# Value products in groups of six units, eight tiles of exponentials and a ring of three score banks in two of a kernel's three attentions

## The chip, the cores and the metric

The kernel runs on one core of one Trainium2 chip. The metric is device time in microseconds (us). Its engines are TensorE (PE; its weight loads are PEld), VectorE (DVE), ScalarE (ACT), GpSimd (POOL) and SyncE (SP, which issues DMAs). Each engine works through its own list of instructions in order and waits on semaphores that the others raise.

## The reference, cut to what matters

Two transformer blocks on 512 tokens of width 1024. The first mixes a differential and a windowed attention ("diff" and "win"). The second has two layers: one with a dense causal attention of 8 heads ("mla"), one with a sparse attention of 16 heads in three branches, compressed, selected and windowed ("nsa"). At this length the selected blocks and the window cover all earlier keys, so the two big branches are plain causal attentions.

```python
# "mla", layer 1: 8 heads, 96 wide, values 64 wide
sc = jnp.einsum('bqhd,bshd->bhqs', q_blk, k).astype(jnp.float32) * scale
sc = jnp.where(kpos[None, :] <= t[:, None], sc, NEG)
p = jax.nn.softmax(sc, axis=-1).astype(v.dtype)
return jnp.einsum('bhqs,bshd->bqhd', p, v)
...
# "nsa", layer 2: 16 heads in 4 groups, three softmaxes for each head
sc = jnp.where(valid, sc, NEG)                      # compressed keys, 31 of them
p_cmp = jax.nn.softmax(sc, axis=-1) * has[:, None]
o_cmp = jnp.einsum('bgrqn,bngd->bqgrd', p_cmp.astype(vc.dtype), vc)
...
p = jax.nn.softmax(sc.reshape(b, G, R, QB, -1), axis=-1).reshape(sc.shape)
o_slc = jnp.einsum('bgrqnl,bgqnld->bqgrd', p.astype(vs.dtype), vs)
...
p = jax.nn.softmax(sc, axis=-1)
o_win = jnp.einsum('bgrqs,bsgd->bqgrd', p.astype(vw.dtype), vw)
return (g_blk[:, :, 0, :, :, None] * o_cmp + g_blk[:, :, 1, :, :, None] * o_slc
        + g_blk[:, :, 2, :, :, None] * o_win)
```

Around the attentions stand projections and feed-forward layers with float32 weights, split into two float16 parts each.

## The kernel before

Most of the time goes to the projections: ACT makes the high float16 part of a weight unit (L1240, `w_hi`), DVE the low part (L1578, `w_lo`), and PE multiplies (L872 to L874). None of that is touched. Three stretches are attentions, written as runs ("mix" for diff and win, "mla", "nsa"). The change is in the last two.

**Slots.** A run is a row of slots, one for each head and branch: 8 in mla, 32 in nsa, where 4 slots make a pair of heads. The work of a slot is done in two halves far apart in the program, because a softmax here needs the row sums before the exponentials that are multiplied with the values are formed.

- First half, *row scores* (`nat_scores`, L963): queries on the partitions, in three chunks of 512, of 384 + 128 and of 256 columns. DVE takes the row maxima (`nat_max`, L1776), ACT the exponentials and row sums, in place in the PSUM bank (`nat_exp`, L1294). ACT then takes the logarithm (`log_sums`, L1331, L1333), DVE splits it into three float16 pieces in a chain of small operations (`split_lse`, L1817 to L1835), PE turns them into rows (`turn_lse`, L1051, here *the turn*), and DVE copies these rows into the query operand (`lse_to_rows`, L1842).
- Second half, *key scores* (`key_scores`, L1005, in *units*): keys on the partitions, so that ACT's exponential (`key_exp`, L1311) gives the final probabilities. The *value products* (`unit_values`, L1035) multiply them in float32 with the values. A unit is 512, 384 + 128 or 256 columns. Two units of the two heads of a pair write the two halves of the output's partitions. In nsa a pair of heads has 12 units and a thirteenth for the compressed branch (scores L999, bias on DVE L1805, product L1027).

**Order.** The order is written out by hand and is the same in form on each engine: `for s in range(-run.ahead, run.n)`, and in slot step s three steps i (a fourth where the thirteenth unit falls). Row scores run `ahead` slots in front (4 in mla, 6 in nsa), so a run opens with a stretch in which PE has row scores alone, here the *lead-in*, and closes with one that has key scores alone. In a step PE issues a unit of key scores, then at i = 1 the turn (every slot in mla, every second slot in nsa), then a chunk of row scores, then the value products that are due: a list of groups of two units, each issued once the last unit of the group lies two behind the current one (L1083). ACT does the unit's exponential, then the row exponential of the step before, then at i = 0 the logarithm. DVE at i = 2 copies the turned rows, takes the chunk's maxima, runs the whole chain of `split_lse`, and in mla and in the last 8 slots of nsa splits one weight unit at the slot's end (L1578), as ACT does (L1240).

**Buffers.** Key scores have three PSUM banks. Row scores alternate between two (`nat_bank`, L768), so chunk c waits until the row exponential of chunk c-2 is done (L966). The turn has a bank of its own, pT[1] (L1049). The exponentials of the units go to four tiles of `tmp`, so `key_exp` of unit u waits for the value product of unit u-4 (L1309).

```python
while now and left[0][-1] <= now[0].u[now[1]] - 2:
    unit_values(left.pop(0))
...
if c >= 2:
    pe.wait_ge(nat_exped, c - 1)
ps = nat_bank(c)
...
if u >= 4:
    act.wait_ge(unit_av, u - 3)
```

Of the kernel before, what the change touches and what calls it, by code (L numbers as in the profile page):

```python
# [29 lines left out]
ACT = mybir.ActivationFunctionType  # L30
# [204 lines left out]
class Run:  # L235
# [26 lines left out]
    def number(self, group, u):  # L262

        if group[0].paired:
# [3 lines left out]
            self.values += [[u + x, u + x + 1] for x in range(0, 6 * b, 2)]  # L268
# [52 lines left out]

RUNS = make_runs()
ALL_SLOTS = [s for r in RUNS.values() for s in r.slots]
# [22 lines left out]
def head_rows(half):  # L346

    return slice(half * HD, (half + 1) * HD)
# [130 lines left out]
def build_program(nc, x_in, stream, consts, params, aux, out):  # L479
    ctx = ExitStack()  # L480
    with ctx:
# [72 lines left out]
        def pair(at, shape):  # L554
# [34 lines left out]
            "p (a b c) -> p a b c", a=NQ, b=4)  # L589
        cqs, at = pair(at, [6, T])  # L590
# [41 lines left out]
        def extra_values(t):  # L632

            if t.kind.name == "diff":
                return vmd[:, t.j, :]
            return vmw if t.kind.name == "win" else vcz[:, 2 * (t.j // 4) + t.j % 2, :]

# [130 lines left out]
        def nat_bank(c):  # L768

            return pT[:, 0, :] if c % 2 else pS[:, 3, :]  # L770
# [67 lines left out]
        def _(pe):  # L838
# [106 lines left out]

            def extra_scores(kind, n, c):

                if c >= 2:
                    pe.wait_ge(nat_exped, c - 1)
# [13 lines left out]
            def nat_scores(t, i):  # L963

                c = t.c + i
                if c >= 2:  # L966
                    pe.wait_ge(nat_exped, c - 1)
# [48 lines left out]
            def unit_values(us):  # L1016
# [9 lines left out]
                if i == len(t.keys):  # L1026
                    pe.matmul(o, extra_values(t), tmp[:, us[0] % 4, :], start=False, stop=True,  # L1027
                              skip_group_check=t.paired).then_inc(unit_av, 1)
                    return
                for n_, (kb, c0, q0, n) in enumerate(t.keys[i]):  # L1030
                    for u in us:
                        t = UNITS[u][0]
                        rows = head_rows(t.half) if t.paired else slice(0, P)
                        new = t.b == 0 and i == 0 and n_ == 0 and (t.paired or t.first)
                        mm = pe.matmul(o[rows, q0:q0 + n], values(t, kb), tmp[:, u % 4, c0:c0 + n], start=new, stop=False,  # L1035
                                       skip_group_check=t.paired)
                        if n_ == len(t.keys[i]) - 1:
                            mm.then_inc(unit_av, 1)

            def turn_lse(t):  # L1040

                pe.wait_ge(lse_split, t.lse + 1)
                if t.lse:
                    pe.wait_ge(lse_rows, t.lse)
# [4 lines left out]
                t16 = pT[:, 1, :].bitcast(F16)  # L1049
# [177 lines left out]
        def _(act):  # L1227
# [69 lines left out]
            def key_exp(t, i):  # L1297
# [11 lines left out]
                if u >= 4:  # L1309
                    act.wait_ge(unit_av, u - 3)  # L1310
                act.activation(tmp[:, u % 4, 0:a.shape[1]], a, ACT.Exp).then_inc(key_exped, 1)  # L1311
# [1105 lines left out]
```

## Time and profile before

| | us |
|---|---|
| median of 3 runs | 2179.01 (2179.01 to 2180.03) |
| the profiled execution, its own time | 2179.95 |
| its span, first to last instruction | 2178.2 |
| PE busy | 2042.6 (94%) |
| DVE busy | 1192.1 (55%) |
| ACT busy | 815.7 (37%) |
| mla: lead-in, then the rest of the run | 20.0 (956.0 to 976.0), 37.1 (to 1013.1) |
| nsa: lead-in with the compressed scores, then the rest | 33.2 (1570.0 to 1603.2), 162.0 (to 1765.2) |
| one pair of heads of nsa, in the middle of the run | 21.35, five times in a row |

Times within the trace count from the first instruction. A timeline row gives a start, a duration, the engine, the line, what is written from what, the size and how many such instructions were merged; in square brackets stands how long the engine was idle just before and what released it. Matmuls overlap in the pipeline, so what a piece of PE's work costs is read from start to start of its neighbours, not from its duration. The profiled execution lies 0.94 above the median, and its own time 1.75 above its span.

### The profile page before, as it was taken

Reading aid. Unit: us, or ns where it says so; the run is one execution under the profiler, and the core shown is the slowest. Engines: PE = TensorE matmul, PEld = TensorE weight load, DVE = VectorE, ACT = ScalarE, POOL = GpSimd, SP = SyncE. Lnnn points to the kernel's source line nnn. Section 1 sums busy time; section 2 is a strip of 40 time slices with the busy share of each in tenths; the row PEclk is TensorE's granted clock in tenths of the full one; section 3 lists DMA queues with packets and bytes.
Section 4 is the critical chain, followed back from the end, with each engine's and each line's share of the span. In section 5 each row is a group of like instructions: output and inputs, shape, how many; then the busy total and the mean of one; then the engine's idle time right before and its main releaser. Section 6 shows DMA issues by size and latency. Waiting matters only on the chain. (4 is left out here: it accounts for less than half of the span.)

```text
span 2178.2 us, 27334 instructions
## 1 busy us (share of the span) xinstructions
PE 2042.6 (94%) x10625; PEld 963.3 (44%) x10625; DVE 1192.1 (55%) x2184; ACT 815.7 (37%) x1481; POOL 38.5 (2%) x40
## 2 busy tenths in 40 slices
PE   7989999999999989979899999899789898999996
PEld 3444444444444434434344444356444443444442
DVE  4956744546554347665676522376555645855222
ACT  3437733323322232446343322234167742422220
POOL 2000000000000002000000000000000000000000
PEclk9979999999999999999999999998879998999998
DMA  6300133324333313313143333235000030433311
GB/s 196 107 1 1 49 97 98 104 68 127 103 107 106 101 59 107 97 30 89 47 127 106 107 101 103 77 104 179 11 1 1 10 99 28 145 105 100 110 44 39
DMA packets 52184, 179.18 MB, mean 82 GB/s; under 512 B 5984, under 2 KB 9696, under 8 KB 51680
## 3 DMA queue, kind: packets, MB, share of 16 engines
q1 hardware_dynamic: 52064, 177.51, 27.1%
q8 instruction: 84, 1.38, 0.3%
q14 instruction: 36, 0.29, 0.0%
HBM read 174.34 MB, written 2.10 MB: 81 GB/s over the span
## 5 line engine op out<-in xcount | busy, mean ns | idle before, releaser
L1578 DVE SCALAR_TENSOR_TENSOR w_lo<-w_raw,w_hi 128x1024 f16<-128x1024 f32 x317 | 385.5, 1219 | 181.8 <-ACT w_hi L1240 161.3
L1240 ACT ACTIVATE w_hi<-w_raw 128x1024 f16<-128x1024 f32 x317 | 331.0, 1049 | 280.6 <-PE pS L874 271.3
L872 PE MATMUL pS<-arena,w_hi 128*128 128x512 f16 x924 | 350.2, 379 | 4.6 <-DVE w_lo L1578 3.1
L872 PE MATMUL pS<-xx,w_hi 128*128 128x512 f16 x928 | 353.1, 380 | 1.4 <-DVE xx L1593 1.4
L873 PE MATMUL pS<-xx,w_hi 128*128 128x512 f16 x928 | 353.0, 380 | 0.0
L874 PE MATMUL pS<-xx,w_lo 128*128 128x512 f16 x928 | 352.9, 380 | 0.0
L873 PE MATMUL pS<-arena,w_hi 128*128 128x512 f16 x924 | 350.2, 379 | 0.0
L874 PE MATMUL pS<-arena,w_lo 128*128 128x512 f16 x924 | 350.2, 379 | 0.0
L1249 ACT ACTIVATE arena<-src 128x512 f16<-128x512 f32 x106 | 66.7, 630 | 325.5 <-DVE src L2151 168.2
L1633 DVE TENSOR_TENSOR tmp<-pS,rs 128x512 f32<-128x512 f32 x98 | 67.5, 689 | 140.1 <-PE pS L874 140.1
L872 PEld LDWEIGHTS pS<-arena,w_hi 128*128 128x128 f16 x924 | 90.5, 98 | 114.4 <-DVE w_lo L1578 3.6
L874 PEld LDWEIGHTS pS<-xx,w_lo 128*128 128x128 f16 x928 | 91.0, 98 | 110.6 <-issue 1.7
L873 PEld LDWEIGHTS pS<-arena,w_hi 128*128 128x128 f16 x924 | 90.4, 98 | 109.1 <-issue 0.6
L874 PEld LDWEIGHTS pS<-arena,w_lo 128*128 128x128 f16 x924 | 90.4, 98 | 109.1
L872 PEld LDWEIGHTS pS<-xx,w_hi 128*128 128x128 f16 x928 | 91.0, 98 | 107.4 <-DVE xx L1593 2.2
L873 PEld LDWEIGHTS pS<-xx,w_hi 128*128 128x128 f16 x928 | 90.9, 98 | 105.3 <-issue 1.5
L1311 ACT ACTIVATE tmp<-pS 128x512 f32<-128x512 f32 (+2 forms) x184 | 97.6, 540 | 53.9 <-PE pS L1013 25.7
L916 PE MATMUL pS<-xx,w_hi 128*128 128x512 f16 x192 | 77.5, 404 | 30.1 <-DVE xx L1593 15.8
L1005 PE MATMUL pS<-arena 128*128 128x512 f16 (+3 forms) x480 | 102.3, 313 | 1.5 <-DVE arena L1842 1.5
L2129 DVE TENSOR_SCALAR xx<-pS 128x512 f32<-128x512 f32 x24 | 16.6, 692 | 144.3 <-PE pS L874 144.3
L1035 PE MATMUL pO<-tmp,arena 128*64 128x256 f32 (+4 forms) x384 | 89.8, 477 | 0.4 <-ACT tmp L1311 0.4
L1776 DVE TENSOR_REDUCE st_max<-pS 128x1 f32<-128x512 f32 (+2 forms) x112 | 55.8, 516 | 57.7 <-PE pS L982 45.3
(317 smaller groups left out, 2763.8 us busy)
## 6 DMA issues: line engine op xcount, KB each, us to landing
w_raw<-in_w SPq DMA_DIRECT2D x317, 512.0 KB, 3.6
X<-in_x SPq DMA_DIRECT2D x1, 2112.0 KB, 8.4
arena<-in_c SPq DMA_DIRECT2D x2, 1024.0 KB, 5.6
out_t<-X SPq DMA_DIRECT2D x8, 256.0 KB, 2.0
arena<-in_h SPq DMA_DIRECT2D x4, 256.0 KB, 15.1
arena<-in_h SPq DMA_DIRECT2D x2, 512.0 KB, 9.3
arena<-in_c SPq DMA_DIRECT2D x2, 256.0 KB, 2.8
arena<-arena SPq DMA_DIRECT2D x4, 128.0 KB, 2.5
```

What stands on the lines that cost most here:

```text
L872: pe.matmul(ps, wh, ah, start=f, stop=False)
L873: pe.matmul(ps, wh, al, start=False, stop=False)
L874: mm = pe.matmul(ps, wl, ah, start=False, stop=l)
L916: pe.matmul(ps, wh, xa[0][:, k, 0:T], start=k == 0, stop=False)
L1005: pe.matmul(ps[:, c0:c0 + n], k[:, ks_], q[:, qs], start=x == 0, stop=False)
L1035: mm = pe.matmul(o[rows, q0:q0 + n], values(t, kb), tmp[:, u % 4, c0:c0 + n], start=new, stop=False, skip_group_check=t.paired)
L1240: act.activation(w_hi[:, u % WR, :], w_raw[:, u % RAW, :], ACT.Copy, scale=WS).then_inc(hi_split, 1)
L1249: act.activation(dst, a, ACT.Identity, scale=scale).then_inc(rhs_hi, 1)
L1311: act.activation(tmp[:, u % 4, 0:a.shape[1]], a, ACT.Exp).then_inc(key_exped, 1)
L1578: dve.scalar_tensor_tensor(out=w_lo[:, u % WR, :], in0=w_raw[:, u % RAW, :], scalar=WS, in1=w_hi[:, u % WR, :], op0=ALU.mult, op1=ALU.subt ...
L1633: dve.tensor_tensor(dst, ps, r[:, 0:T], ALU.mult).then_inc(evicted, 1)
L1776: ins = dve.tensor_reduce(stat(st_max, t)[:, x:x + 1], nat_bank(c)[:, c0:c0 + n], AX.X, ALU.max, negate=True)
```

## The change

- In mla and nsa the value products are issued in groups of six units instead of two (diff and win keep theirs). Inside a group the pairs follow each other with no other matmul between them, and the group waits once, for the exponential of its last unit.
- In mla and nsa the exponentials have eight tiles instead of four: the four of `tmp` and four in a part of the arena whose contents are no longer needed (`cqs` in mla, `cbias` in nsa). Unit u waits for the product of unit u-8.
- In mla and nsa the row scores and the turn share three banks, pS[3], pT[0] and pT[1], in one ring in the order in which PE issues them. Each waits for the reader of what stood in its bank three places earlier: the row exponential of a chunk, or the copy of a turned row. `mix` keeps two banks and one.

```diff
@@ number
-            self.values += [[u + x, u + x + 1] for x in range(0, 6 * b, 2)]
+            n = 2 if group[0].kind.name == "win" else 6
+            self.values += [list(range(u + x, u + x + n)) for x in range(0, 6 * b, n)]
@@ new
+def make_rings():
+    nat, turn, free = {}, {}, {}
+    for name, r in RUNS.items():
+        own = {"nat": 0, "turn": 0}
+        last = {}
+
+        def place(table, key, done, which):
+            if name == "mix":
+                b = key % 2 if which == "nat" else 2
+            else:
+                b = (own["nat"] + own["turn"]) % 3
+            own[which] += 1
+            table[key] = b
+            free[which, key] = last.get(b)
+            last[b] = done
+
+        for _, _, c in r.pre:
+            place(nat, c, ("nat", c + 1), "nat")
+        for s in range(-r.ahead, r.n):
+            nxt, t = r.at(s + r.ahead), r.turned(s)
+            for i in range(r.steps(s)):
+                if i == 1 and t is not None:
+                    place(turn, t.lse, ("turn", t.lse + 1), "turn")
+                if nxt is not None and i < len(nxt.nat):
+                    place(nat, nxt.c + i, ("nat", nxt.c + i + 1), "nat")
+    return nat, turn, free
@@ tiles and banks
+        def p_more(t):
+
+            return {"mla": [p_mla[:, n, :] for n in range(4)], "nsa": [cbias[:, n, :] for n in range(4)]}.get(t.kind.name, [])
...
-            return pT[:, 0, :] if c % 2 else pS[:, 3, :]
+            return ring_bank(NAT_BANK[c])
+
+        def ring_bank(b):
+
+            return pT[:, b - 1, :] if b else pS[:, 3, :]
@@ nat_scores, turn_lse
-                if c >= 2:
-                    pe.wait_ge(nat_exped, c - 1)
+                ring_free("nat", c)
...
-                if t.lse:
-                    pe.wait_ge(lse_rows, t.lse)
+                ring_free("turn", t.lse)
@@ unit_values
+                for x in range(0, len(us), 2):
+                    i = UNITS[us[x]][1]
+                    for n_, (kb, c0, q0, n) in enumerate(t.keys[i]):
+                        for u in us[x:x + 2]:
@@ key_exp
-                if u >= 4:
-                    act.wait_ge(unit_av, u - 3)
+                n = len(p_more(t)) + 4
+                if u >= RUNS["mix" if t.kind.name in ("diff", "win") else t.kind.name].u0 + n:
+                    act.wait_ge(unit_av, u - n + 1)
```

PE in nsa, from the end of the row scores of an even slot to the turn in the odd slot after it. L974 and L982 are row scores, L1005 and L1013 key scores, L1035 value products, L1051 the turn (L1024, L1032, L1055, L1063, L1087 and L1102 in the changed kernel). Before:

```order
L974 MATMUL pS<-arena 128x256 x2
L982 MATMUL pS<-causal,identb 128x128
L1005 MATMUL pS<-arena 128x384 x2
L1013 MATMUL pS<-identb,causal 128x128
L1005 MATMUL pS<-arena 128x128 x2
L1013 MATMUL pS<-identb,causal 128x128
L974 MATMUL pT<-arena 128x512 x2
L982 MATMUL pT<-causal,identb 128x128
L1035 MATMUL pO<-tmp,arena 64x512 x2
L1005 MATMUL pS<-arena 128x256 x2
L1013 MATMUL pS<-identb,causal 128x128
L1051 MATMUL pT<-identh,lse_cols 128x128 x4
```

The same place in the changed kernel:

```order
L1024 MATMUL pS<-arena 128x256 x2
L1032 MATMUL pS<-causal,identb 128x128
L1055 MATMUL pS<-arena 128x384 x2
L1063 MATMUL pS<-identb,causal 128x128
L1055 MATMUL pS<-arena 128x128 x2
L1063 MATMUL pS<-identb,causal 128x128
L1024 MATMUL pT<-arena 128x512 x2
L1032 MATMUL pT<-causal,identb 128x128
L1055 MATMUL pS<-arena 128x256 x2
L1063 MATMUL pS<-identb,causal 128x128
L1102 MATMUL pT<-identh,lse_cols 128x128 x4
```

The pair of value products has left this place; the rest is as it was. PE in nsa where a pair of heads begins, after its first unit, changed kernel (before, the one row `64x256 x2` stood there):

```order
L1024 MATMUL pT<-arena 128x512 x2
L1032 MATMUL pT<-causal,identb 128x128
L1087 MATMUL pO<-tmp,arena 64x512
L1087 MATMUL pO<-arena 64x512
L1087 MATMUL pO<-arena 64x384 x2
L1087 MATMUL pO<-arena 64x128 x2
L1087 MATMUL pO<-arena 64x256
L1087 MATMUL pO<-tmp,arena 64x256
L1055 MATMUL pS<-arena 128x512 x2
L1063 MATMUL pS<-identb,causal 128x128
```

Six units of the heads before stand here in one piece; the other six stand after the eighth unit. PE in mla, changed kernel, from the turn of slot 2 to the third chunk of row scores of that slot:

```order
L1102 MATMUL pT<-identh,lse_cols 128x128 x4
L1024 MATMUL pS<-arena 128x384 x3
L1032 MATMUL pS<-causal,identb 128x128
L1024 MATMUL pS<-arena 128x128 x3
L1032 MATMUL pS<-causal,identb 128x128
L1087 MATMUL pO<-tmp,xx 64x512 x2
L1087 MATMUL pO<-tmp,xx 64x384 x2
L1087 MATMUL pO<-tmp,xx 64x128 x2
L1087 MATMUL pO<-arena,xx 64x256 x2
L1055 MATMUL pS<-arena 128x384 x3
L1063 MATMUL pS<-identb,causal 128x128
```

All six units now stand ahead of that third chunk; before, only the `64x256 x2` did between these two places.

## Rows read from the trace of the kernel before

**Rows 1.** The page's first line.

```profile
span 2178.2 us, 27334 instructions
```

**Rows 2.** Busy time in stretches: engine busy (instructions), PEclk granted clock, DMA share.

```profile
1687.13:1708.48 21.35, 19.42 (x145) 10.01 (x143) 12.47 (x40) 15.97 (x51) 0.00 (x0) 1.00 0.00 1
...
956.00:976.00 20.00, 12.30 (x73) 6.63 (x71) 13.49 (x40) 11.59 (x36) 0.00 (x0) 0.83 0.03 11
976.00:1013.10 37.10, 35.67 (x280) 19.75 (x280) 26.92 (x87) 31.22 (x82) 0.00 (x0) 1.00 0.30 86
1570.00:1603.20 33.20, 20.65 (x144) 10.46 (x144) 22.63 (x60) 15.31 (x51) 0.00 (x0) 0.50 0.00 0
```

**Rows 3.** Timeline of PE in nsa, within one pair of heads.

```profile
1692.38 0.22 PE L982 MATMUL pS<-causal,identb 128*128 128x128 bf16 x1
...
1693.93 0.61 PE L974 MATMUL pT<-arena 128*128 128x512 f16 x2 [0.78 <-ACT pT L1294]
1694.37 0.22 PE L982 MATMUL pT<-causal,identb 128*128 128x128 bf16 x1
1694.52 1.08 PE L1035 MATMUL pO<-tmp,arena 128*64 128x512 f32 x4
1695.53 0.39 PE L1005 MATMUL pS<-arena 128*128 128x256 f16 x2
...
1695.82 0.39 PE L1051 MATMUL pT<-identh,lse_cols 128*128 128x128 f16 x4
...
1697.13 0.39 PE L974 MATMUL pT<-arena 128*128 128x256 f16 x2
```

**Rows 4.** Timeline of DVE, then of ACT, at the same place.

```profile
1692.64 0.42 DVE L1776 TENSOR_REDUCE st_max<-pS 128x1 f32<-128x256 f32 x1 [0.98 <-PE pS L982]
1692.98 0.16 DVE L1817 TENSOR_TENSOR lse<-st_max,lse_l 128x12 f32<-128x12 f32 x1
...
1694.87 0.68 DVE L1593 SCALAR_TENSOR_TENSOR xx<-pO,xx 128x512 f16<-128x512 f32 x1
1695.47 0.68 DVE L1776 TENSOR_REDUCE st_max<-pT 128x1 f32<-128x512 f32 x1
...
1696.30 0.66 ACT L1294 ACTIVATE pT<-pT,st_max 128x512 f32<-128x512 f32 x1
```

**Rows 5.** Timeline at the end of mla, ACT and PE.

```profile
1010.02 1.06 ACT L1240 ACTIVATE w_hi<-w_raw 128x1024 f16<-128x1024 f32 x1
...
1010.97 1.15 ACT L1311 ACTIVATE tmp<-pS 128x512 f32<-128x512 f32 x3
...
1011.62 1.52 PE L1035 MATMUL pO<-tmp,xx 128*64 128x384 f32 x12
```

**Rows 6.** Timeline of PE in the lead-in of nsa: two turns and a wait between.

```profile
1590.94 0.61 PE L1051 MATMUL pT<-identh,lse_cols 128*128 128x128 f16 x4 [0.65 <-DVE lse_cols L1829]
...
1594.52 1.03 PE L974 MATMUL pS<-arena 128*128 128x512 f16 x2 [1.37 <-ACT pS L1294]
...
1600.43 0.61 PE L1051 MATMUL pT<-identh,lse_cols 128*128 128x128 f16 x4 [0.65 <-DVE lse_cols L1829]
```

**Rows 7.** Timeline of PE in mla: third row chunks of slots 1 to 3, turn.

```profile
985.46 0.50 PE L974 MATMUL pT<-arena 128*128 128x256 f16 x3
...
991.53 0.49 PE L974 MATMUL pS<-arena 128*128 128x256 f16 x3
...
997.40 0.50 PE L974 MATMUL pT<-arena 128*128 128x256 f16 x3 [0.36 <-ACT pT L1294]
...
1000.32 0.39 PE L1051 MATMUL pT<-identh,lse_cols 128*128 128x128 f16 x4
...
1001.22 0.66 PE L1005 MATMUL pS<-arena 128*128 128x384 f16 x3
```

**Rows 8.** Busy time in two neighbouring stretches of the lead-in of mla, columns as in rows 2.

```profile
969.30:972.60 3.30, 1.69 (x13) 0.70 (x10) 2.74 (x12) 1.92 (x8) 0.00 (x0) 1.00 0.00 0
972.70:976.00 3.30, 2.85 (x16) 1.84 (x16) 1.69 (x5) 1.36 (x5) 0.00 (x0) 0.50 0.00 0
```

More of the change, by code:

```diff
@@ L636, in extra_values, with p_tile @@
             return vmw if t.kind.name == "win" else vcz[:, 2 * (t.j // 4) + t.j % 2, :]
+        def p_more(t):
+            return {"mla": [p_mla[:, n, :] for n in range(4)], "nsa": [cbias[:, n, :] for n in range(4)]}.get(t.kind.name, [])
+        def p_tile(t, u):
+            more = p_more(t)
+            n = (u - RUNS[t.kind.name].u0) % 8 if more else u % 4
+            return tmp[:, n, :] if n < 4 else more[n - 4]
         def passes(t):
@@ L944, in norm, with ring_free @@
                 norm_spread(name, meta)
+            def ring_free(which, key):
+                last = RING_FREE[which, key]
+                if last is not None and last[0] == "nat":
+                    pe.wait_ge(nat_exped, last[1])
+                elif last is not None:
+                    pe.wait_ge(lse_rows, last[1])
             def extra_scores(kind, n, c):
-                if c >= 2:
-                    pe.wait_ge(nat_exped, c - 1)
+                ring_free("nat", c)
                 ps = nat_bank(c)
@@ L1026, in unit_values @@
                 if i == len(t.keys):
-                    pe.matmul(o, extra_values(t), tmp[:, us[0] % 4, :], start=False, stop=True,
+                    pe.matmul(o, extra_values(t), p_tile(t, us[0]), start=False, stop=True,
                               skip_group_check=t.paired).then_inc(unit_av, 1)
                     return
[L1030 to L1038, printed above, removed]
+                for x in range(0, len(us), 2):
+                    i = UNITS[us[x]][1]
+                    for n_, (kb, c0, q0, n) in enumerate(t.keys[i]):
+                        for u in us[x:x + 2]:
+                            t = UNITS[u][0]
+                            rows = head_rows(t.half) if t.paired else slice(0, P)
+                            new = t.b == 0 and i == 0 and n_ == 0 and (t.paired or t.first)
+                            mm = pe.matmul(o[rows, q0:q0 + n], values(t, kb), p_tile(t, u)[:, c0:c0 + n], start=new, stop=False,
+                                           skip_group_check=t.paired)
+                            if n_ == len(t.keys[i]) - 1:
+                                mm.then_inc(unit_av, 1)
             def turn_lse(t):
                 pe.wait_ge(lse_split, t.lse + 1)
-                if t.lse:
-                    pe.wait_ge(lse_rows, t.lse)
+                ring_free("turn", t.lse)
                 if t.kind.name in ("diff", "win"):
@@ L1308, in key_exp @@
                         a = pS[:, u % 3, 0:c0 + n]
[L1309 to L1311 removed]
+                n = len(p_more(t)) + 4
+                if u >= RUNS["mix" if t.kind.name in ("diff", "win") else t.kind.name].u0 + n:
+                    act.wait_ge(unit_av, u - n + 1)
+                act.activation(p_tile(t, u)[:, 0:a.shape[1]], a, ACT.Exp).then_inc(key_exped, 1)
             def exp_joined(t):
```

9 lines of the change are left out of this document (5 added, 4 removed).

## The prediction

> **What bounds the kernel now.** I read the page first. The span is 2178.2 us [rows 1], and PE is busy for 94% of it, so only what PE issues or waits for counts. The projections are not touched. That leaves the two attentions, and there I read the busy time by stretches [rows 2], then the timeline of PE, and for each of PE's waits the timelines of DVE and ACT.
>
> The reader is to see three things in rows 2. In one pair of heads in the middle of nsa (21.35 us) PE is busy 19.42, ACT 15.97 and DVE 12.47. PE is nearly full and no other engine is, so the change, which lets PE wait less, looks right at first sight. In the lead-ins, PE is busy for about 60% (12.30 of 20.00, 20.65 of 33.20), at a granted clock below full speed: there PE waits for a chain, not for itself. In the rest of mla DVE and ACT are busy for 26.92 and 31.22 of 37.10.
>
> Now the timeline of nsa [rows 3]. The third chunk of row scores of an even slot ends its issue at 1692.38 + 0.06 = 1692.44; the third chunk of the next, odd slot starts at 1697.13. In these 4.69 us PE's own work is 2.35 without the value products (0.54 + 0.49 + 0.28 for the next score units, 0.22 for the turn, 0.54 + 0.28 after it, each from start to start of such pieces in this timeline), and the pair of value products takes 1.10 (1694.37 to 1695.53, less 0.06 for the last small matmul). The remaining 1.21 is waiting: 0.94 before the row scores at 1693.93 (the timeline's bracket shows 0.78 of it) and 0.27 before those at 1697.13.
>
> What ends this stretch is a chain on other engines [rows 4]: DVE begins the maxima 0.20 after 1692.44, `split_lse` runs from 1692.98 to 1694.87, the low part of the output before is 0.60, the maxima of the first chunk of the odd slot start only then, at 1695.47, and last 0.68; ACT's exponential of that chunk follows (1696.30), and at 1697.13, 0.83 after its start, the chunk that reuses its bank may begin. Added without the small wait on ACT: 0.20 + 0.34 + 1.89 + 0.60 + 0.68 + 0.04 + 0.83 = 4.58, as good as the 4.69 measured. **PE is almost full there because the work fits into a chain of fixed length, not because the work is the bound.**
>
> **The change part by part.**
>
> *Groups of six.* A group costs PE something at its edges: of the 1.10 for the 512 columns above, four passes of 512 columns at 2.4 GHz are 0.853, so 0.25 is entry and exit. Two groups that happened to touch at the end of mla took 1.52 [rows 5], the 1.08 of one alone [rows 3] plus 0.44, which is the 0.427 of the columns of the second: inside a group nothing is added. So each group joined saves 0.25. In nsa six groups a pair of heads become two: 1.0 for each of eight pairs. In mla twelve become four: 2.0 in all. The whole group of six then takes 2.13 + 0.25 = 2.38 in one piece, in nsa after the first and after the eighth unit of a pair of heads.
>
> *What the groups uncover.* The stretch of 4.69 above loses its value products (the first pair of rows in the section on the change). The chain is as long as before, so the 1.10 turns into waiting: 4.58 - 2.35 = 2.23 instead of 1.21. It shows as a new wait of some 1.3 before the turn, which needs the last operation of `split_lse`, and one of about 0.9 before the third chunk. The second such stretch of a pair of heads has no output part in its chain (3.98): waiting 1.63, where before the timeline has 0.94 + 0.27 = 1.21.
>
> *The ring of three.* It takes away the waits for a bank where the chunk three places earlier is an older one: 0.94 twice and 0.33 once a pair of heads. It does not take away the one that ends the stretch: between the first and the third chunk of an odd slot the ring holds the first chunk, the turn, the second, and the third comes back to the first one's bank. It waits for the same exponential as before.
>
> *The sum for a pair of heads in nsa.* Before: 21.35 less 2.75 of waits (0.94, 0.27, 0.33, 0.94, 0.27) is 18.60 of work. After: 18.60 - 1.00 + 2.23 + 1.63 = 21.46. Five of them: +0.5. The first pair of heads loses 0.5 of bank waits before its first stretch and gains half a pair's change: -0.2. In the seventh, weight splits lengthen the chain by 1.1 and the turn at its end waits 0.7 more: +0.5 with its brackets. The last pair, with score units alone, waits for ACT, whose weight splits stand between exponentials: 0. I bound each by the brackets alone (-1.0) and by a group's own value time (+1.1).
>
> *The lead-in of nsa.* Here the ring helps. From turn to turn it is 9.49 us [rows 6]; the wait of 1.37 before the chunk at 1594.52 is for a bank, and behind it stand chunk, maxima, exponential, third chunk, maxima, `split_lse`, turn. With the third bank that chunk waits for the copy of the turned row instead, some 0.6 earlier, and the third chunk of the slot no longer for the first one's exponential (0.53 and what follows it): I get 8.2, so -1.3. The three slots before it are the same without a turn: by the same steps the turn at 1590.94 comes 2.6 earlier. Together -3.9, bounds -1.5 (only the two bank waits named) and -5.5.
>
> *mla.* The lead-in gains 1.2 in the same way. Then [rows 7] the third chunks start at 985.46, 991.53 and 997.40. In mla the weight split on DVE, 1.2, is part of the chain. To 985.46 and from 991.53 to 997.40 the chain decides before and after: 0. From 985.84 to 991.53, 5.69, the group of six stands in the way (last pair of rows on the change): 6.5, +0.8. After 997.78 come two score units (1.42), the turn and the rest of the values until 1001.22, 3.44 in all. Now the turn waits 0.8 for `split_lse` and 2.38 of values stand behind it: 4.87, +1.4. These hold the brackets saved. At the end [rows 5] ACT does a weight split (0.95 from start to start) and then the last exponentials; the last group of six needs the last of them, where before two pairs covered the time. That is 1.8 of waiting less 1.0 of brackets: +0.9. mla: -1.2 + 0.8 + 1.4 + 0.9 = +1.9, bounds -1 and +4.
>
> *Eight tiles.* They carry no term of their own: unit u waits for the product of u-8, which PE has issued before the scores of unit u. Without them the groups could not be formed.
>
> *Sum.* -3.9 - 0.2 + 0.5 + 0.5 + 1.9 = -1.2 us. The profiled execution is 0.94 above the median, and the sum is a difference, so it goes onto the median: 2179.0 - 1.2 = **2177.8**.
>
> **The rivals.**
>
> *Rival 1, PE's work is the bound.* If the chain gave way (for instance because the row maxima no longer queue behind `split_lse`), 1.0 of brackets and 2.2 of bank waits would go from each of some six pairs of heads: -19, and with the lead-ins 2155. For it: PE at 19.42 of 21.35 [rows 2]. Against it: DVE's order is not changed, and rows 4 show each step of the chain starting at the end of the one before. A half way, in which the turn's wait and the chain are half as long as I have them, gives 2165 to 2173.
>
> *Rival 2, slower by the clock.* In the lead-in of mla PE worked 1.69 of 3.30 us at full clock, with its longest rest about a microsecond, and in the stretch behind it the granted clock was 0.50 [rows 8]. My new waits, 1.3 and 0.9 about a microsecond apart, make a stretch of about that emptiness, twice a pair of heads, where before each had 1.21 of waits in 4.69 and the clock stayed at 1.00 [rows 2]. What follows each is dense score work and a group of six, so a fall to 1.2 GHz for one such stretch costs some 1.6 us. It decides from the point where the two waits of a stretch fall together. If it happens in half of the fourteen stretches, +11: 2189; once or twice, +2 to +3, which leaves the forecast's class.
>
> The Trainium skill, "TensorE: Matmul & The Clock Gate", section "Why this matters for your kernels", warns of single idle gaps longer than any I expect. By that rule the clock would stay at 2.4 GHz and rival 2 would have no cost; the rows of mla's lead-in speak against reading it so, since no single rest in them was that long.
>
> *Rival 3, the lead-in gives nothing* (DVE's own maxima and chains turn out to fill it): the sum becomes +2.7 and the time 2181.7, still within the class.
>
> **How the numbers follow.** The forecast with its bounds (2173 to 2183): 0.55. The half way of rival 1: 0.13; rival 1 itself: 0.10. Rival 2 with several falls: 0.15; a little of both 2 and 3, just past the bound: 0.07. A measurement of this kernel can tell about 0.2%, 4.4 us, from no change, so "same" is 2174.6 to 2183.4. The forecast holds nearly all of it: same 0.54; faster 0.24 (rival 1 in both forms); slower 0.22. The range leaves out rival 1 in full and the far end of rival 2: 2166 to 2187.
>
> **What the changed profile would show.** Right: the distance between the compressed scores of neighbouring pairs of heads stays at 21.2 to 21.7; the turn in nsa waits 1.2 to 1.4 for DVE's last piece of `split_lse`, which it hardly did; the waits of row scores for ACT before first chunks are gone and those before third chunks of odd slots are longer; the lead-in of nsa is 3 to 5 shorter; a group of six takes 2.4; mla is longer after its lead-in. Wrong: a distance under 20.5 means that the chain was not the bound; granted clock of 0.50 inside nsa is rival 2; single bursts well above 2.4 would mean that units do pay between each other. What would most easily make the number wrong is the chain's length, since 0.1 of it counts thirteen times.

## The result, and the profile after

| | before | after |
|---|---|---|
| median, runs | 2178.85 us, 17 (2176.93 to 2180.16) | 2183.3 us, 17 (2181.18 to 2184.64) |
| ratio, 95% interval | | 1.002 (1.0012 to 1.0027) |
| span of the profiled execution | 2178.2 | 2181.5 |

The changed kernel is slower by 4.45 us. The forecast was 2177.8, so -1.2, with a range of 2166 to 2187: the time lies inside the range and on the other side of no change, 5.5 us above the forecast. Two of the six executions of the run without the ring, below, took about 3100 us at a mean granted clock of 0.65, and one of the kernel before beside it took 3592 us at 0.55; they are left out of the times and ratios.

First the page's first line and busy time by stretches, as in [rows 1, 2] (columns as there): mla behind its lead-in, the lead-in of nsa, in it the distance of two turns, then in nsa a normal pair of heads, the one of the five middle pairs that is longer, and the seventh pair.

```profile
span 2181.5 us, 27317 instructions
```

```profile
974.05:1018.23 44.18, 35.37 (x281) 20.35 (x281) 27.64 (x88) 31.10 (x83) 0.00 (x0) 0.99 0.25 73
1577.61:1602.04 24.43, 13.69 (x80) 6.45 (x81) 20.08 (x56) 14.17 (x49) 0.00 (x0) 0.77 0.00 1
1593.24:1599.93 6.69, 3.65 (x29) 1.91 (x29) 5.57 (x20) 4.82 (x18) 0.00 (x0) 1.00 0.01 2
1640.30:1661.69 21.39, 18.30 (x144) 10.35 (x143) 12.44 (x41) 15.71 (x50) 0.00 (x0) 1.00 0.00 1
1683.09:1706.16 23.07, 19.98 (x144) 10.95 (x143) 12.43 (x41) 15.93 (x50) 0.00 (x0) 0.93 0.00 1
1727.57:1749.60 22.03, 18.43 (x121) 9.35 (x119) 12.24 (x37) 15.19 (x42) 0.00 (x0) 0.85 0.17 49
```

A normal pair of heads takes 21.39 with PE busy for 18.30, where before it was 21.35 with 19.42 [rows 2]: PE does less and the pair is as long. One pair takes 23.07 and the seventh 22.03, and of the pairs of heads these two alone have a granted clock below 1.00. The timeline of PE shows where the freed time went; these are the turn, the third chunk of the odd slot, the start of the group of six (here also called a burst) and the key scores behind it:

```profile
1671.32 0.40 PE L1102 MATMUL pT<-identh,lse_cols 128*128 128x128 f16 x4 [1.14 <-DVE lse_cols L1881]
...
1673.29 0.39 PE L1024 MATMUL pS<-arena 128*128 128x256 f16 x2 [0.66 <-ACT pS L1345]
...
1675.68 0.64 PE L1087 MATMUL pO<-arena 128*64 128x512 f32 x1
...
1677.99 0.50 PE L1055 MATMUL pS<-arena 128*128 128x384 f16 x2
```

In place of the waits of [rows 3] stand 1.14 before the turn, for the last piece of `split_lse` (DVE, L1881), and 0.66 before the third chunk. The other turn of the pair waits 1.14 as well (at 1681.44), and the burst takes 2.31 from its start to the next piece.

The whole difference, measured between like marks of the two traces (the first row score of a run, its first key unit, the compressed scores of each pair of heads, the last value product), beside the terms of the forecast:

| stretch | forecast | before | after | difference |
|---|---|---|---|---|
| mla, lead-in | -1.2 | 20.12 | 18.70 | -1.42 |
| mla, to the first piece behind the values of the fourth turn | +2.2 | 25.05 | 27.73 | +2.68 |
| mla, to the last value product | +0.9 | 11.54 | 14.65 | +3.11 |
| nsa, lead-in | -3.9 | 28.88 | 24.43 | -4.45 |
| nsa, first pair of heads | -0.2 | 19.81 | 16.86 | -2.95 |
| nsa, the next five | +0.5 | 106.75 | 108.67 | +1.92 |
| nsa, seventh | +0.5 | 18.41 | 22.03 | +3.62 |
| nsa, last, to its last value product | 0 | 16.38 | 18.77 | +2.39 |

Of the first pair's -2.95, 1.06 is the mark alone: a burst that stood ahead of the compressed scores now stands behind them (turn to compressed scores 2.71 before, 1.65 after), and the last row gives it back. The table sums to +4.9; the rest of the program, which the change does not touch, is 1.6 shorter in this profiled execution, and the medians say +4.45.

### The profile page after: what moved, and what is told of

It reads as the page before. It is cut to its first block and busy times, and to the rows that moved or that the text cites. A ratio compares the mean times of both kernels' runs of the same rounds, so it can differ in the third digit from the quotient of the medians.

```text
span 2181.5 us, 27317 instructions
## 1 busy us (share of the span) xinstructions
PE 2031.9 (93%) x10625; PEld 965.9 (44%) x10625; DVE 1192.1 (55%) x2184; ACT 813.5 (37%) x1481; POOL 38.5 (2%) x40
## 5 line engine op out<-in xcount | busy, mean ns | idle before, releaser
L1300 ACT ACTIVATE arena<-src 128x512 f16<-128x512 f32 x106 | 66.8, 630 | 325.5 <-DVE src L2203 168.2
L1055 PE MATMUL pS<-arena 128*128 128x512 f16 (+3 forms) x480 | 103.8, 318 | 4.6 <-DVE arena L1894 3.1
L1828 DVE TENSOR_REDUCE st_max<-pT 128x1 f32<-128x512 f32 (+3 forms) x140 | 68.1, 507 | 53.0 <-PE pT L1032 41.6
L1645 DVE SCALAR_TENSOR_TENSOR arena<-src,arena 128x512 f16<-128x512 f32 x106 | 72.9, 688 | 26.6 <-ACT arena L1300 26.4
L1024 PE MATMUL pT<-arena 128*128 128x512 f16 (+3 forms) x302 | 69.7, 333 | 18.7 <-ACT pT L1345 14.8
```

What stands on the lines that cost most here:

```text
L1024: pe.matmul(ps[:, c0:c0 + n], q[:, qs], k[:, ks_], start=x == 0, stop=False)
L1055: pe.matmul(ps[:, c0:c0 + n], k[:, ks_], q[:, qs], start=x == 0, stop=False)
L1300: act.activation(dst, a, ACT.Identity, scale=scale).then_inc(rhs_hi, 1)
L1645: dve.scalar_tensor_tensor(out=dst, in0=a, scalar=scale, in1=h, op0=ALU.mult, op1=ALU.subtract).then_inc(rhs_ready, 1)
L1828: ins = dve.tensor_reduce(stat(st_max, t)[:, x:x + 1], nat_bank(c)[:, c0:c0 + n], AX.X, ALU.max, negate=True)
```

## The experiments

Times are medians, ratios are to runs of the kernel before beside them (their medians are 2178.39 to 2179.06). Where a stretch is compared between two traces, one profiled execution stands against another. Short diffs are against the changed kernel unless said otherwise.

### The ring without the groups

```diff
-            n = 2 if group[0].kind.name == "win" else 6
+            n = 2
```

> Groups of two units everywhere, as before the change; the ring of three banks and the eight tiles stay. Theory (a chain on DVE and ACT sets the length of the stretches around each compressed turn in nsa, and groups of six only take PE's own work out of them): both lead-ins keep their gain (-4.5 in nsa, -1.4 in mla), the mla rest falls back from 42.4 to 36.6 or less, the clock does not fall in nsa, and a pair of heads falls below 21.35, to about 20.2, since the waits for a bank (0.94 and 0.33) go where the chain is not yet the limit. Time about 2167 (2163 to 2173). Rival (fewer group edges are what the change lives from, and the ring is worth only its lead-ins): a pair of heads at 21.35 or more and about 2173 to 2177. If neither lead-in gains, the ring is not their cause: 2179.

Measured: **2165.8 us** (2164.6 to 2167.37), ratio to before 0.9942 (0.9929 to 0.9956). The pair of heads is where the theory had it. Busy time of one pair of heads, and the wait that is left in it:

```profile
1653.25:1673.45 20.20, 19.32 (x144) 9.96 (x142) 12.44 (x40) 15.80 (x51) 0.00 (x0) 1.00 0.01 2
```

```profile
1663.15 0.39 PE L1024 MATMUL pS<-arena 128*128 128x256 f16 x2 [0.67 <-ACT pS L1345]
```

Neither turn of the pair waits. So the groups of six, which take 1.0 of PE's work out of each pair of heads, are what makes the changed kernel slow: 2183.3 - 2165.8 = 17.5, with what they cost through the clock in it.

### The groups without the ring

```diff
-            if name == "mix":
+            if True:
```

> Groups of six and eight tiles stay, the ring goes: row scores alternate between two banks and the turn has its own. Theory: the lead-ins lose their gain (28.9 in nsa again, 20.1 in mla), the pair of heads stays at 21.4 since the same chain sets it, and the ends of mla and nsa stay longer. Time about 2189 (2186 to 2193). Rival (the lead-in gain comes from elsewhere, or the ring itself costs in the steady part): 2183 or less.

Measured: **2189.17 us** (2187.97 to 2190.42; ratio 1.0046, 1.0031 to 1.0061). The lead-in of nsa is 28.88 again and the pair of heads 21.82. I had said 21.4; in the rows two waits of 0.78 for a bank are back, each with 0.19 before its turn behind it, and that they make the 0.4 is read from these rows and was not tried. In this trace the five middle pairs are all of one length and the seventh takes 19.24, at a clock of 1.00. The lead-in of mla, 19.07, did not go back to 20.12, but up to its first turn it did: 12.23 against 12.34 before and 11.14 with the ring. What lies behind is its last stretch, in which the clock fell before and did not here. So the ring is worth 1.1 in mla's lead-in, and the comparison of two single traces owes the rest to the clock.

### Groups of six in nsa alone

```diff
-            n = 2 if group[0].kind.name == "win" else 6
+            n = 6 if group[0].kind.name == "nsa" else 2
```

> Groups of two in mla, groups of six in nsa, ring and tiles as in the changed kernel. Theory (in mla the burst of six holds back the output parts on ACT and DVE, and behind these the copy of the turned row that opens the next pair): mla's rest falls from 42.4 to 36.6 or less, its lead-in stays 18.7, nsa is as in the changed kernel. Time about 2177.5 (2175 to 2180). Rival (the ring, not the groups, costs in mla): mla's rest stays above 40 and the time near 2183.

Measured: **2175.3 us** (2173.36 to 2177.52), ratio 0.9984 (0.9976 to 0.9993). mla's rest is 36.78, so the burst costs 5.6 there and the ring nothing. The time fell by 8.0, which is more. In nsa, whose instructions are the same as in the changed kernel, the fall of the clock in the middle did not come (21.40 five times) and the seventh pair took 20.07 instead of 22.03, together 3.6 less. But the clock was lower at nsa's start. These are the distance of two turns in the lead-in, the first pair of heads and the seventh:

```profile
1585.82:1593.19 7.37, 5.07 (x29) 2.52 (x29) 5.60 (x20) 4.94 (x18) 0.00 (x0) 0.77 0.01 2
1595.30:1613.62 18.32, 15.74 (x120) 9.17 (x121) 10.71 (x37) 14.62 (x48) 0.00 (x0) 0.91 0.00 1
1720.62:1740.69 20.07, 17.08 (x121) 9.17 (x119) 12.34 (x37) 15.19 (x42) 0.00 (x0) 0.91 0.17 53
```

The first two took 6.69 and 16.86 at 1.00 in the changed kernel, and the lead-in and first pair together 41.29 against 43.42 here. From its first row score to its last value product nsa is only 1.5 shorter, and another 1.7 of the 8.7 between the two spans lies outside the two attentions, in code that the edit does not touch.

### The same groups, one unit later

```diff
-                        while now and left[0][-1] <= now[0].u[now[1]] - 2:
+                        while now and left[0][-1] <= now[0].u[now[1]] - (3 if now[0].kind.name == "nsa" else 2):
```

> As the changed kernel, but in nsa a group of six goes out once its last unit lies three behind the current one instead of two. So the first group of a pair of heads stands behind the third chunk of an even slot, where a chain stretch opens, and the second still before one. Theory (the chain bounds, PE waits there): the 2.38 of that group fills the waits of its stretch (1.63), and a pair of heads falls from 21.40 to about 19.8, seven times, which also leaves fewer falls of the clock: about 2172 (2168 to 2176). Rival (the whole of PE's work and its group edges bound, or the exponentials run out of tiles behind the later group): the pair of heads stays within 21.2 to 21.6 and the time is 2181 to 2185. If it is the output parts that then come late, the distance grows instead.

Measured: **2163.84 us** (2162.78 to 2164.41), ratio 0.9932 (0.9918 to 0.9945). A pair of heads takes 19.31, less than I had said (19.8). The burst now stands right behind the third chunk of an even slot, where the chain begins, and the next turn (1672.97) does not wait; the other stretch still does:

```profile
1664.16 0.40 PE L1102 MATMUL pT<-identh,lse_cols 128*128 128x128 f16 x4 [0.23 <-DVE lse_cols L1881]
1666.13 0.39 PE L1024 MATMUL pS<-arena 128*128 128x256 f16 x2 [0.66 <-ACT pS L1345]
1669.34 0.64 PE L1087 MATMUL pO<-arena 128*64 128x512 f32 x1
...
1672.97 0.39 PE L1102 MATMUL pT<-identh,lse_cols 128*128 128x128 f16 x4
```

The first wait shrank from 1.14 to 0.23 too, since the thirteenth unit's product (0.92) also goes out one unit later and now stands in that stretch: that is what I had not counted. With the same groups, the same work and the same chain, 19.5 us hang on where the products of nsa stand (some 4.5 of it through the clock, below). This is the strongest evidence that the changed kernel is slow because its bursts stand outside the chain's stretches.

### A shorter chain

```diff
-                    if n == 2:
+                    if n == (1 if t.kind.name in ("mla", "nsa") else 2):
                         ins.then_inc(lse_split, 1)
```

> The changed kernel without the third float16 piece of the log sums in mla and nsa (two small DVE operations and their links of each split are left out, 0.45 us; the third column keeps what stood there). PE's work is the same. Theory (the chain sets the length of both stretches): a pair of heads falls from 21.40 by 2 x 0.45 to 20.5, the turn's wait from 1.14 to 0.7, and mla's rest by some 2; time about 2174 (2171 to 2177). Rival (PE's own work, or the burst of six itself, bounds): a pair of heads stays at 21.3 to 21.4 and the time at 2181 to 2184.

Measured: **2173.91 us** (2172.89 to 2175.51), and 20.55 for a pair of heads: 0.85 gone where two times 0.45 were taken out of DVE. The turn's wait:

```profile
1667.51 0.40 PE L1102 MATMUL pT<-identh,lse_cols 128*128 128x128 f16 x4 [0.69 <-DVE lse_cols L1881]
```

PE's work was not touched. The chain sets the length. Of the 9.4 by which the time fell, the chain in the five middle pairs is 4.3; in its trace the fall of the clock in their midst, 1.67, did not come either. mla did not give the 2 that I expected in its rest (43.32, longer than 42.38); in its last 17.7 us the granted clock was 0.90, where the changed kernel has 1.00. Its lead-in is 1.5 shorter (17.22), at a clock of 0.90 against 0.83, so that gain is in part the clock's too.

### More work for PE, to hold the clock

```diff
             def turn_lse(t):
 
-                pe.wait_ge(lse_split, t.lse + 1)
                 ring_free("turn", t.lse)
+                if t.kind.name == "nsa" and t.s >= 5:
+                    q, k = passes(t)[0]
+                    for _ in range(3):
+                        pe.matmul(ring_bank(TURN_BANK[t.lse]), k[:, 0:P], q[:, 0:T], start=True, stop=True)
+                pe.wait_ge(lse_split, t.lse + 1)
```

In the changed kernel the two falls look like this (busy time as above; each time the stretch with the waits, then the one behind it; under it the waits of the second from the timeline of PE):

```profile
1691.60:1694.80 3.20, 1.41 (x14) 0.97 (x15) 3.03 (x10) 2.59 (x8) 0.00 (x0) 1.00 0.02 5
1695.00:1698.20 3.20, 3.20 (x12) 1.43 (x11) 1.12 (x2) 2.33 (x10) 0.00 (x0) 0.50 0.00 0
1736.00:1739.10 3.10, 1.11 (x13) 0.74 (x12) 2.93 (x8) 2.68 (x7) 0.00 (x0) 1.00 0.01 3
1739.50:1745.90 6.40, 5.60 (x18) 2.11 (x19) 4.42 (x15) 4.74 (x14) 0.00 (x0) 0.50 0.47 118
```

```profile
1737.21 0.40 PE L1102 MATMUL pT<-identh,lse_cols 128*128 128x128 f16 x4 [1.14 <-DVE lse_cols L1881]
...
1738.46 0.50 PE L1024 MATMUL pT<-arena 128*128 128x384 f16 x2 [0.85 <-ACT pT L1345]
```

> The changed kernel with three matmuls of 512 columns more in nsa before each turn's wait from the first key unit on (14 turns). They write to the bank that the turn overwrites, and take 0.64 of the 1.14 that PE waits there. Theory (the granted clock fell twice in nsa because the two waits of a stretch fall together, 1.67 and some 1.9 us): with the wait half filled it stays at full speed, a pair of heads is 21.40 each time, the seventh about 20.1, and the time is about 2180.5 (2179.5 to 2182). Rival (the falls have another cause): they come as often as before, and the time stays at 2183.3 (2182 to 2185). If the turn's wait is shorter than I take it, each filler adds and the time is above 2185.

Measured: **2178.99 us** (2177.53 to 2181.42), so 4.3 less than the changed kernel with 42 matmuls more. The same two pairs of heads in its trace (21.41 and the seventh), the clock at 1.00:

```profile
1703.17:1724.58 21.41, 19.94 (x152) 10.77 (x150) 12.44 (x41) 15.71 (x50) 0.00 (x0) 1.00 0.00 1
1724.58:1743.82 19.24, 17.06 (x127) 8.95 (x125) 12.24 (x37) 15.19 (x42) 0.00 (x0) 1.00 0.19 55
```

The seventh went from 22.03 to 19.24, not to 20.1: the 20.07 that I took from the run with groups of six in nsa alone held a short fall of its own (clock 0.91 over that pair). So the two falls cost 1.67 and 2.79 in the changed kernel's trace, 4.46; the other stretches of nsa differ by at most 0.2 between these two traces, and the median agrees. The seventh pair of the run without the ring, which has no filler, took 19.24 at full clock as well. One caution: the profiled execution (2177.53) is the shortest of the eleven, and five of them lie at 2180.4 to 2181.4; what the clock did in those no trace shows.

### The output parts of mla one slot later

```diff
-                        e = run.ended(s - 1)
+                        e = run.ended(s - 1 - (run is RUNS["mla"]))
                         if i == 2 and e is not None and e.kind.name != "diff":
                             y_hi(e, dst[e.kind.name])
```

and the same for `y_lo`. Near the end of mla the changed kernel has a wait of 1.95 that was not there before. DVE, then PE:

```profile
1003.88 0.69 DVE L1645 SCALAR_TENSOR_TENSOR arena<-pO,arena 128x512 f16<-128x512 f32 x1 [1.50 <-ACT arena L1300]
1004.82 1.23 DVE L1630 SCALAR_TENSOR_TENSOR w_lo<-w_raw,w_hi 128x1024 f16<-128x1024 f32 x1 [0.25 <-ACT w_hi L1291]
1005.97 0.41 DVE L1894 COPY arena<-pT 32x512 f16<-32x512 f16 x1
...
1006.43 0.82 PE L1055 MATMUL pS<-arena 128*128 128x512 f16 x3 [1.95 <-DVE arena L1894]
```

The key scores of the last pair need the turned row (turn at 1003.71). Its copy stands on DVE behind the low part of an output and a weight split, and these wait for ACT, which got to the high part (L1300) late, since it stood behind an exponential whose scores PE issued after the burst.

> The changed kernel with the high and low output parts of mla (ACT and DVE) one slot later, so that on DVE the copy of the last turned row no longer stands behind a low part that waits for the burst of six. Theory (that row copy is what PE waits for, 1.95, before the key scores of the last pair): the wait shrinks to about 1.4, where the weight split, still in front of the copy and itself behind exponentials and the split's high part on ACT, becomes the limit; mla's rest goes from 42.3 to 41.2 to 41.9, time 2182.5 (2181 to 2184). Rival (the wait has nothing to do with the outputs): 1.9 or more remain and nothing moves.

Measured: **2178.26 us** (2177.11 to 2180.05). The wait became

```profile
1005.02 0.82 PE L1055 MATMUL pS<-arena 128*128 128x512 f16 x3 [1.58 <-DVE arena L1894]
```

and mla's rest 41.01, a little better than the range I gave. So the low part carries 0.4 of the wait. That the weight split carries the rest fits its place in the rows and was not tried. The wait of PE for the last exponentials, at the very end of mla, fell by 0.5 too (1.71 to 1.23). The time is 5.0 below the changed kernel, of which mla explains 1.4. nsa, which was not edited, is 1.5 shorter, as in the run with groups of six in nsa alone: 21.40 five times and 20.07 in the seventh, but 25.12 and 18.32 in the lead-in and the first pair. Most of the rest, 1.9, lies between the two attentions and is not explained. So the falls do not follow from nsa's code alone. Its start in time is what differs; that this decides was not tested.

### How much of nsa's lead-in is the clock

Before, the lead-in ran at 0.50 to its end [rows 2]; in the changed kernel it is at 1.00 in its second half (6.69 from turn to turn, in the table of stretches above). This run adds work to the kernel before, nothing else:

```diff
+                if t.kind.name == "nsa" and 1 <= t.s < 6:
+                    q, k = passes(t)[0]
+                    for _ in range(2):
+                        pe.matmul(pS[:, 1, :], k[:, 0:P], q[:, 0:T], start=True, stop=True)
                 if c >= 2:
                     pe.wait_ge(nat_exped, c - 1)
...
+                if t.kind.name == "nsa" and t.s < 5:
...
+                    for _ in range(3):
...
                 pe.wait_ge(lse_split, t.lse + 1)
```

> The kernel before the change, with matmuls of 512 columns added in nsa's lead-in (two ahead of each row-score chunk's wait, three ahead of each turn's), which write to a bank of key scores that is free there. The question is how much of the changed kernel's shorter lead-in is the ring and how much the clock: before, the lead-in ran at a granted clock of 0.50 to its end, in the changed kernel at 1.00 for its second half, and there turn to turn fell from 9.49 to 6.69. Theory (half and half): the added work raises the clock to 1.00 behind the first slots; from turn to turn two first chunks and two third ones are 0.44 and 0.25 shorter, so 9.49 becomes 8.1 (7.8 to 8.6), the lead-in 28.88 becomes 26.5 to 27.5, and the time falls by 1.5 to 2 in spite of the work added. Rival (the clock is of no account, the ring alone did it): turn to turn stays at 9.4 or more, as does the lead-in, or it grows by the work added.

Measured: **2176.74 us** (2174.94 to 2178.11), 1.65 less than before by the medians (2178.39 beside it), ratio 0.9993 (0.9984 to 1.0003), so not certain as a time. In the trace it is plain; the stretches are from the first row score to the first turn, and from it to the second:

```profile
1571.68:1588.47 16.79, 11.89 (x57) 5.21 (x57) 11.12 (x30) 7.82 (x27) 0.00 (x0) 0.73 0.00 0
1588.47:1596.91 8.44, 6.78 (x44) 3.21 (x44) 5.69 (x20) 4.94 (x18) 0.00 (x0) 1.00 0.01 2
```

From turn to turn 9.49 became 8.44, and the lead-in 27.77, short of the 26.5 to 27.5 expected. So of the 2.80 that the changed kernel gained between its turns, at least 1.05 is the clock and at most 1.75 the ring, since the added work can only lengthen what the clock shortens; of the lead-in's 4.45, at least 1.1 is the clock.

### Tiles, and better versions

> Groups of two and the ring of three banks, but four tiles of exponentials as before the change: the ring alone. Theory (the tiles carry no term of their own): the same as with groups of two, ring and eight tiles, a pair of heads of 20.2, time 2165.8 (2164 to 2168). Rival (part of that gain is the tiles': exponentials wait less for value products): a pair of heads at 20.5 or more and 2168 or more.

Edit: groups of two everywhere, and `p_more` returns an empty list. Measured: **2165.82 us**, 20.20 for a pair of heads, the same as with eight tiles. The ring alone, about thirty lines, is worth 13 us.

> Groups of two in mla, and in nsa groups of six that go out one unit later (behind the third chunk for the first group of a pair of heads). Ring and tiles as in the changed kernel. Theory (the two effects are separate): mla's rest 36.8 instead of 42.2, pair of heads in nsa 19.3, time 2163.8 - 5.6 = about 2158 (2156.5 to 2160). Rival (they share a cause, such as exponential tiles or the clock): less than 3 is gained over the run with the later groups alone, 2161 or more.

Both edits shown above together. Measured: **2158.4 us** (2157.57 to 2160.12), as the sum of the two said.

> As the run before it, but in nsa the twelve units go out as six, two and four: six behind the third chunk that opens one chain stretch, two a little later, and four with the thirteenth behind the third chunk that opens the other; the high and low output parts (ACT and DVE) go one slot later, out of that stretch. Theory (both stretches of a pair of heads are as long as their chain, 3.98, unless PE has more to do in them): now both are filled (2.35 + 2.38, and 2.35 + 0.28 + 1.6), the work of 18.60 less 0.75 for group edges is all that is left, and a pair of heads takes 18.0 to 18.5 instead of 19.3. Time about 2151 (2147 to 2156). Rival (ACT becomes late: its exponentials wait for the tiles of the later groups): a pair of heads at 19.0 or more and waits of PE for ACT, time 2157 or more.

```diff
+                self.values += [list(range(u + x, u + y)) for x, y in ((0, 6), (6, 8), (8, 12), (12, 13))]
+                self.due += [u + 8, u + 13, u + 15, u + 15]
```

Measured: **2157.11 us**, 19.05 for a pair of heads: a miss. I had priced the thirteenth unit's product at 0.28; the trace has it at 0.92, from 1678.14 to the next piece at 1679.06 in the kernel of the run above. With it the second stretch holds more than its chain, so filling it further gains nothing. The rival (PE waits for ACT) named the time but not the cause: in a pair of heads PE has two waits of 0.16 left.

> Groups of two in mla; in nsa groups of six one unit later, and the output parts of nsa (high on ACT, low on DVE) one slot later, out of the chain stretch of the even slot. Theory (in that stretch PE still waits 0.23 before the turn and 0.67 before the third chunk, and the low part's 0.60 stands in its chain before the row maxima): a pair of heads falls from 19.30 to 18.7 (18.6 to 18.9), the turn's wait stays, and the time is 2158.4 - 4 = 2154 (2153 to 2156). Rival (PE's work is the bound by now, near the 19.05 of the run with six, two and four): 19.0 or more and 2156 to 2158.

The edit is that of the later outputs above with `RUNS["nsa"]`, on groups of two in mla and the later groups of six in nsa. Measured: **2155.84 us** (2155.71 to 2157.17), ratio to before 0.9896 (0.988 to 0.9911), the fastest of all, 27.5 below the changed kernel. One pair of heads:

```profile
1650.82:1669.64 18.82, 18.28 (x144) 10.34 (x143) 12.42 (x41) 16.04 (x51) 0.00 (x0) 1.00 0.01 2
```

PE's 18.28 of busy time is that of the changed kernel (18.30), in 18.82 instead of 21.39. Time and distance lie inside the theory's ranges (2153 to 2156, 18.6 to 18.9), the time at their edge.

## Why the prediction was right or wrong, step by step

**What bounds the kernel: right.** "The work fits into a chain of fixed length" was the reading of [rows 3, 4], and it held three ways: the chain shortened by 0.90 shortened the pair of heads by 0.85; work taken out of the stretch (groups of six) gave nothing back; work moved into it gave 2.1 per pair. The steady pair of heads was forecast at 21.46 and measured 21.40; the turn's wait was forecast at 1.2 to 1.4 and is 1.14; the wait before the third chunk was forecast at about 0.9 and is 0.66; a burst was forecast at 2.38 and is 2.30 (987.55 to 989.85 in mla). Rival 1 fell: it needed the chain to give way.

**Rival 2, the clock: this is the step that failed.** I gave it 0.15 with several falls and 0.07 with a few, and put no term for it in the sum. There were two falls in the profiled execution, and they cost 4.46 of the 5.5 us between forecast and result. The place was named rightly (two waits that fall together, the granted clock at 0.50 behind them), and the first price too (1.6 said, 1.67 measured). The second price was too low: in the seventh pair the waits stand closer (1.14 and 0.85 one behind the other) and the clock stayed down for twice as long, 2.79. That the waits bring the falls about is shown by the fillers; why only two of the fourteen stretches fell is not, and the same nsa code fell less in two other kernels. The Trainium skill, "TensorE: Matmul & The Clock Gate", section "Why this matters for your kernels", warns only of single gaps longer than these; by that reading the clock would have stayed up. The trace does not agree: no single wait there was over 1.14. My own reading of [rows 8] said so beforehand, and I let it weigh too little.

**The lead-in of nsa: right in size (-3.9 said, -4.45 measured), half right in cause.** The steps counted only bank waits at the half clock. The ring did at most 1.75 of the 2.80 between two turns; the rest is that the clock came up. The sum had no term for that gain either, and it varies: with the same nsa code the two turns were 7.37 apart at a clock of 0.77, and 6.69 at 1.00.

**The first pair of heads: too small.** -0.2 said, -1.9 measured when the mark is taken out. Before, it still had bank waits in its first slots and a clock of 0.94 over its first 7.15 us; in the changed kernel's trace the clock is 1.00 over the whole pair. With the same code it took 18.32 at a clock of 0.91, so 1.5 of the gain is the clock's in this one trace.

**mla up to the fourth turn's values: right.** The two places of the sum were 5.69 to 6.5 and 3.44 to 4.87; measured 6.65 (from 983.98 to 990.63) and 4.90 (from 996.88 to 1001.78).

**The end of mla: the second step that failed.** The burst at the very end was right (1.8 of waiting said, 1.71 measured):

```profile
1014.43 1.08 PE L1087 MATMUL pO<-tmp,xx 128*64 128x512 f32 x4 [1.71 <-ACT arena L1363]
```

What the sum left out is the wait of 1.95 for the turned row at 1006.43. I had followed what waits for values on PE alone. Following what is queued behind each delayed instruction on every engine would have found it: burst, exponential and high part on ACT, low part and weight split on DVE, row copy, key scores.

**The last pair in nsa: wrong.** 0 said, +2.39 measured, 1.3 without the mark. I had argued that this pair waits for ACT anyway. Before, PE's waits in this pair add up to 1.29 (0.43 and 0.86, both at value products); with bursts it waits for ACT's exponentials before it can issue scores, 2.45 in all:

```profile
1758.32 0.61 PE L1055 MATMUL pS<-arena 128*128 128x512 f16 x2 [1.47 <-ACT arena L1363]
...
1764.55 1.04 PE L1049 MATMUL pS<-arena 128*128 128x512 f16 x4 [0.98 <-ACT arena L1363]
```

Another wait of this kind, 0.80 at 1749.60, ends where the last pair begins and counts in the seventh. That two-unit products used to cover such waits is read from the rows and was not tested by a run of its own.

**Eight tiles: right.** They carry no time of their own, shown with groups of two.

Without the falls the forecast would have been close, and partly by luck: the changed kernel with the clock held up takes 2178.99, against 2177.8 said. The parts beyond that (end of mla +2.2, last pair +1.3, first pair -1.7, lead-in of nsa -0.6) mostly cancelled, and the last two are in part the clock's gain.

## What to carry to other kernels

Where an engine is busy for nine tenths of a stretch and still not the bound, taking work off it gains nothing; first find the chain whose length the stretch has, then move work into it, beginning right behind the instruction that starts it. Joining groups into a burst saves their edges (0.25 for each group joined here) and holds back everything that is queued behind it on the other engines; the same bursts in nsa, one unit later, made the kernel 19.5 us faster. And short waits that fall together are to be priced with the clock, also when none of them is long, as a term with its own bounds: here it cost 4.5 in one place and gave back about 2 in another.

## What the runs showed of the hardware that I had not expected

- The granted clock of PE fell to 0.50 behind a stretch of 3.1 us in which PE worked 1.11 us and its longest wait was 1.14, and 42 added matmuls, which compute nothing, made the kernel 4.3 us faster.
- With the same nsa code the clock fell in two pairs of heads in one kernel and in one, briefly, in another that differs in mla only (23.07 and 22.03 against 21.40 and 20.07), while the lead-in and the first pair went the other way (41.29 against 43.42). A comparison of two traces that differ by a few microseconds must look at the clock of each stretch first, even where the code of the stretch is the same.
- A product of 512 columns in float32 for the thirteenth unit took 0.92. Two units of 512 columns, one for each half of the output's partitions, took 1.10 with both edges of their group [rows 3]; so the thirteenth, which fills all partitions alone, costs about as much as two others.
